# Logit matmuls of two attention units side by side on different TensorE row groups, in a fused two-block transformer kernel

## What is computed

```python
def _token_mixers(h, ...):
    proj = h @ w_in
    a, b, c, d = jnp.split(proj, ...)
    o_a = _mixer_window(a, sink, slopes[:4])      # "win": 4 heads of 64, bias by distance
    o_b = _mixer_mla(b, ...)                      # "mla": 4 heads of 96
    o_c = _mixer_axial(c, ax_q_norm, ax_k_norm)   # "ax": 4 heads of 64
    o_d = _mixer_diff(d, ...)                     # "dif": 4 heads, two maps of 32 each, bias by distance
    return jnp.concatenate([o_a, o_b, o_c, o_d], axis=-1) @ w_out
# every mixer: s = q @ k.T * scale (+ bias); p = softmax(s); o = p @ v
```

## Time and profile before

| | |
|---|---|
| runs (3) | 1475.52, 1479.99, 1492.61 us; median 1479.99 us |
| profiled execution | 1476.0 us |
| its span, first to last instruction | 1474.7 us |
| mean granted TensorE clock | 0.968 |
| busy: TensorE, VectorE, ScalarE, GpSimd | 1389.5, 845.7, 657.8, 93.0 us |

### The profile page before, as it was taken

The page is one execution under the profiler, slowest core; times in us unless marked ns, Lnnn a source line. Parts: engine busy times, 40 slices in busy tenths (PEclk is TensorE's granted clock), DMA queues, the critical chain, the costliest instruction groups (busy, mean ns, idle before and its releaser), DMA issues.

```text
span 1474.7 us, 23294 instructions
## 1 busy us (share of the span) xinstructions
PE 1389.5 (94%) x9838; PEld 1290.4 (88%) x9838; DVE 845.7 (57%) x1141; ACT 657.8 (45%) x939; POOL 93.0 (6%) x137
## 2 busy tenths in 40 slices
PE   6798799999899999998899999899999999899997
PEld 6687799998799998888889999899998878799997
DVE  3787655666655547546554546655457446655545
ACT  5556345445434443555244344443343545344332
POOL 1233000000000000500000000000001400000000
PEclk9998889999999999999899999999999999899999
DMA  7233276667556563421575566566655232376561
GB/s 225 87 95 120 86 214 186 186 187 206 164 180 196 177 186 104 136 94 37 141 220 180 173 195 204 155 189 184 198 153 155 91 114 69 104 209 191 181 197 52
DMA packets 301201, 229.36 MB, mean 156 GB/s; under 512 B 13083, under 2 KB 283818, under 8 KB 301098
## 3 DMA queue, kind: packets, MB, share of 16 engines
q1 hardware_dynamic: 301082, 227.88, 51.3%
q10 hardware_dynamic: 16, 0.00, 0.0%
HBM read 226.80 MB, written 1.05 MB: 155 GB/s over the span
## 4 chain that ended last, share of the span: by engine, by line
PE 82%; DVE 10%; ACT 5%; DMA 1%; issue 1%; POOL 0%; SPq 0%; DVEq 0%; ACTq 0%
PE bank L796 24%; PE bank L797 24%; PE bank L798 24%; DVE lo_gu L1638 3%; PE bank L1213 2%; PE bank L1183 2%; ACT hi_gu L1307 2%; PE bank L1193 1%; PE bank L1000 1%; DVE stats L1665 1%; DMA st_gu<-in_w_out 1%; PE bank L806 1%; PE bank L1010 1%; DVE xTl L1653 1%; DVE x L1659 1%
## 5 line engine op out<-in xcount | busy, mean ns | idle before, releaser
L796 PE MATMUL bank<-xTh,hi_gu 128*128 128x256 f32 x1864 | 533.2, 286 | 9.6 <-DVE big L1843 5.8
L797 PE MATMUL bank<-xTl,hi_gu 128*128 128x256 f32 x1864 | 531.2, 285 | 0.0
L798 PE MATMUL bank<-xTh,lo_gu 128*128 128x256 f32 x1864 | 531.1, 285 | 0.0
L1638 DVE TENSOR_TENSOR lo_gu<-st_gu,hi_gu 128x2048 fp32r<-128x2048 f32 (+2 forms) x146 | 324.1, 2222 | 169.6 <-ACT hi_gu L1307 169.6
L796 PEld LDWEIGHTS bank<-xTh,hi_gu 128*128 128x128 f32 x1864 | 361.8, 194 | 13.6 <-issue 7.8
L797 PEld LDWEIGHTS bank<-xTl,hi_gu 128*128 128x128 f32 x1864 | 361.8, 194 | 1.7
L798 PEld LDWEIGHTS bank<-xTh,lo_gu 128*128 128x128 f32 x1864 | 361.5, 194 | 0.0
L1307 ACT ACTIVATE hi_gu<-st_gu 128x2048 fp32r<-128x2048 f32 (+3 forms) x147 | 269.5, 1837 | 20.7 <-DMA st_gu<-in_ffn_w_val 10.5
L796 PE MATMUL bank<-hi_dn,actTh 128*128 128x512 f32 x436 | 171.7, 394 | 9.3 <-DVE actTl L1773 7.3
L797 PE MATMUL bank<-lo_dn,actTh 128*128 128x512 f32 x436 | 170.3, 391 | 0.0
L798 PE MATMUL bank<-hi_dn,actTl 128*128 128x512 f32 x436 | 169.8, 389 | 0.0
(11 more groups left out here) (261 smaller groups left out, 1496.8 us busy)
## 6 DMA issues: line engine op xcount, KB each, us to landing
st_gu<-in_ffn_w_gu SPq DMA_DIRECT2D x176, 512.0 KB, 5.1
st_dn<-in_ffn_w_down SPq DMA_DIRECT2D x109, 512.0 KB, 6.3
st_gu<-in_w_in SPq DMA_DIRECT2D x23, 1024.0 KB, 5.4
st_gu<-in_w_out SPq DMA_DIRECT2D x12, 1024.0 KB, 5.2
st_gu<-in_ffn_w_gate SPq DMA_DIRECT2D x21, 512.0 KB, 5.0
st_gu<-in_ffn_w_val SPq DMA_DIRECT2D x21, 512.0 KB, 6.3
st_gu<-in_w_in SPq DMA_DIRECT2D x10, 512.0 KB, 4.8
gb<-in_ln_g SPq DMA_DIRECT2D x6, 512.0 KB, 6.6
```

Of the source, the lines that this page charges most:

```text
L796: pe.matmul(o, lhs[0], rhs[0], start=start, stop=False, **kw)
L797: pe.matmul(o, lhs[0], rhs[1], start=False, stop=False, **kw)
L798: return pe.matmul(o, lhs[1], rhs[0], start=False, stop=stop, **kw)
L1638: i = dve.tensor_tensor(low, staged, high.bitcast(F32), ALU.subtract)
```

## The change

`UNITS` now runs over pr inside m: units u and u+1 (u even) are the same tokens with neighbouring pr, so they lie in different row groups, except in mla. `logits(u)` now issues both units u and u+1. It first waits for the banks of both, then issues the four bias matmuls, then the products in the order (z=0, u), (z=0, u+1), (z=1, u), (z=1, u+1). It is called at even steps only. Nothing else is moved: `weighted`, `probabilities` and the loops of the other engines keep their places.

```diff
-UNITS = [(kind, m, pr) for kind in KINDS for pr in range(4 if kind == "dif" else 2) for m in range(M)]
+UNITS = [(kind, m, pr) for kind in KINDS for m in range(M) for pr in range(4 if kind == "dif" else 2)]
...
                 def logits(u):
-                    kind, m, pr = UNITS[u]
-                    b, ts = bank[u % LOGIT_BANKS], slice(m * P, (m + 1) * P)
-                    if u < LOGIT_BANKS:
-
-                        wait_projected(pe, l, 1, 0)
-                        wait_projected(pe, l, 0, 1)
-                    else:
-                        pe.wait_ge(exp_ok.sem, exp_ok[l, u - LOGIT_BANKS])
+
+                    for v in (u, u + 1):
+                        if v < LOGIT_BANKS:
+
+                            wait_projected(pe, l, 1, 0)
+                            wait_projected(pe, l, 0, 1)
+                        else:
+                            pe.wait_ge(exp_ok.sem, exp_ok[l, v - LOGIT_BANKS])
...
                     for z in range(2):
-                        if kind == "mla":
-                            q_, k_ = mlaq[0:96, 2 * pr + z, ts], mlak[0:96, 2 * pr + z, :]
...
-                        t = pe.matmul(b[:, z * S:(z + 1) * S], q_, k_, start=not biased, stop=True, skip_group_check=biased)
-                    t.then_inc(logits_ok.sem, logits_ok.one((l, u)))
+                        for v in (u, u + 1):
+                            pr = UNITS[v][2]
+                            if kind == "mla":
+                                q_, k_ = mlaq[0:96, 2 * pr + z, ts], mlak[0:96, 2 * pr + z, :]
...
+                            t = pe.matmul(bank[v % LOGIT_BANKS][:, z * S:(z + 1) * S], q_, k_, start=not biased, stop=True, skip_group_check=biased)
+                            if z == 1:
+                                t.then_inc(logits_ok.sem, logits_ok.one((l, v)))
...
                 logits(0)
                 half(4, 0)
-                logits(1)
                 half(4, 1)
                 units = len(UNITS)
                 for s in range(units + 1):
-                    if s + 2 < units:
+                    if s + 2 < units and s % 2 == 0:
                         logits(s + 2)
```

More of the change, by code:

```diff
@@ L1167, in logits @@
                         pe.wait_ge(qk_copied.sem, qk_copied[l, "mla", 1, 2])
+                    kind, m, _ = UNITS[u]
+                    ts = slice(m * P, (m + 1) * P)
                     biased = kind in ("win", "dif")
                     if biased:
-                        for z in range(2):
-                            pe.matmul(b[:, z * S:(z + 1) * S], slopes[:, 2 * pr + z if kind == "win" else 4 + pr, :],
-                                      distances[:, m, 0 if kind == "win" else 1, :], start=(z == 0), stop=False, skip_group_check=True)
@@ L1184, in logits @@
-                    t.then_inc(logits_ok.sem, logits_ok.one((l, u)))
+                        for v in (u, u + 1):
+                            pr = UNITS[v][2]
+                            for z in range(2):
+                                pe.matmul(bank[v % LOGIT_BANKS][:, z * S:(z + 1) * S], slopes[:, 2 * pr + z if kind == "win" else 4 + pr, :],
+                                          distances[:, m, 0 if kind == "win" else 1, :], start=(z == 0), stop=False, skip_group_check=True)
+                    for z in range(2):
+                        for v in (u, u + 1):
+                            pr = UNITS[v][2]
+                            if kind == "mla":
+                                q_, k_ = mlaq[0:96, 2 * pr + z, ts], mlak[0:96, 2 * pr + z, :]
+                            elif kind == "dif":
+                                rows_ = slice(32 * pr, 32 * pr + 32)
+                                q_, k_ = difq[rows_, z, ts], difk[rows_, z, :]
+                            else:
+                                rows_ = slice(64 * pr, 64 * pr + 64)
+                                q_, k_ = (winq, axq)[kind == "ax"][rows_, z, ts], (wink, axk)[kind == "ax"][rows_, :]
+                            t = pe.matmul(bank[v % LOGIT_BANKS][:, z * S:(z + 1) * S], q_, k_, start=not biased, stop=True, skip_group_check=biased)
+                            if z == 1:
+                                t.then_inc(logits_ok.sem, logits_ok.one((l, v)))
```

## The result

The changed kernel runs at 1463.39 us (median of 20 runs), the kernel before at 1475.18 us in the same comparison: a ratio of 0.9919, 95% interval 0.9899 to 0.9938. That is 11.8 us or 0.8% faster, where 7.6 us were forecast. The profiled execution took 1463.38 us, its span is 1462.0 us (1474.7 before). The chain that ended last still has these shares by engine

A forecast was written before the change was run, and what follows sets the result against it. TensorE was taken as the bound (82% of the chain), except at the step-11 wait. Per layer 6.7 us kept less 2.9 of new waits gives 3.8, 7.6 in two layers: 1470.0 us, range 1460 to 1485.

The forecast's parts named there:

- A pair costs one unit: Logits on TensorE: two units in different row groups run side by side, eight records lasting as long as four, 1.05 us.
- the bound of no overlap: Upper bound for a pair of logits: eight records one after another, 1.91 us; as a rival, no change, chance 0.13.
- The wait in step 11 takes back two pairs: TensorE's wait behind output chunk 3's load grows to about 5 or 6 us; units 10 to 13 lose 2.3 us saved.
- the rival that more would stay: Step-11 wait falls, new waits are hidden, half clock behind it goes; about 1460 us, over 1% faster, chance 0.14.
- The new waits: Odd steps: TensorE waits for the copy of probabilities in steps 1, 13, 15, 17; 2.9 us per layer, even steps nothing.
- The sum: Per layer 6.7 us kept less 2.9 of waits gives 3.8, two layers 7.6; time taken as 1470.0 us.
- The clock in the mla steps: Rival: waits in mla keep TensorE at 1.2 GHz to step 17, some 13 us per layer, 1498 us; chance 0.07.
- The rival's sentence that the waits would vanish at half clock: In the falling-clock case, steps last twice as long and the waits of 2.2 us vanish; the rival's chance 0.07.
- the reading that the full clock was back at 679 us: Kernel before, after the step-11 wait of 3.7 us: half clock follows, full clock back at 679 us after gapless TensorE work.

The follow-up runs named there:

- mla_single: Changed kernel with the logits of mla (units 16 to 19) issued one at a time at each step, as before; 1461.29 us, ratio to before 0.9907.
- late_chunk_single: Kernel before with output chunk 3 moved later (high part from step 9 to 12, low part to 13); 1465.34 us, ratio 0.9922.
- ax_second_pair_single: Changed kernel with the logits of units 4 and 5 (ax) issued singly in steps 2 and 3; 1478.88 us, ratio to before 1.0015.
- order_alone: Kernel before with only the new UNITS order, still one unit of logits at every step; 1474.48 us, ratio 1.0000.
- pairs_same_rows: Changed kernel's pairs at even steps, but UNITS in the old order, so both units share a row group; 1476.69 us, ratio to before 1.0014.
- aabb_in_pair: Changed kernel, but inside each pair both halves of unit u come first, then both of u+1; 1465.8 us, ratio to before 0.9939.
- ax_single_mla_single: Changed kernel with the logits of units 4 and 5 and of all mla units issued singly; 1465.51 us, ratio to before 0.9928.

## Why the prediction was right, point by point

- **A pair costs one unit.** Right, and exact: 1.07 us where 1.05 was taken, 1.89 without row groups where the bound of no overlap was 1.91. It came from a routine of other shape in the same trace, by subtracting 0.19 us for each change of row groups. That subtraction carried the reading: the 0.42 us of `scores` as they stand are just four records of 0.107 one behind the other, and what backed the overlap besides was only the stretch with four records in flight. No run measures what a change costs inside `scores`. The Trainium skill, "TensorE: Matmul & The Clock Gate", Part 3, has a pack in different row groups last about as long as one of its matmuls. The traces here agree, at 256 float32 columns and two units: 1.07 us against 1.05.
- **The wait in step 11 takes back two pairs.** Right: steps 8 to 12 took 22.1 us before and after, and the pairs save 1.05 us there once the load is out of the way. The wait grew to 4.74 us, a little short of the "5 or 6" forecast. The chain kept its length (14.0 against 14.1). So the rival that more would stay, by the half clock behind that wait, falls: that half clock lasts 6.8 us in both kernels. More did stay than was counted, but in another place.
- **The new waits.** Right in place and size: from start to start 0.69 in step 1, 0.4 to 0.5 in step 13, 0.85 in steps 15 and 17, none at even steps. The profile's own idle times are shorter (0.45, 0.25, 0.69), since part of the latency is filled. mla_single takes the last ones away.
- **The sum.** Too small: 6.1 and 6.3 us per layer against 3.8. Of the difference, 1.5 to 1.6 per layer are the half-clock stretch of step 3 (8.22 us for the step with it in the kernel before, 6.70 without it in late_chunk_single). The prediction read the clock only from 635 us on and never priced this stretch, which stands at 625 to 629 us of the trace that it had. Without it the gain would have been some 8.6 us (an estimate: 11.8 less twice 1.6), close to the 7.6. The remaining 0.7 to 0.8 are small terms: 0.15 in the pairs of steps 0 and 1, 0.1 in each pair of ax, 0.3 in steps 8 to 13 together, and 0.16 in the mla steps, which lost 1.56 and not 1.72. The time itself, 1463.4 against the 1470.0 taken, was off by 6.6: 4.2 from the gain, and 2.4 from the base, which was set between the profiled execution and a median of three runs (1479.99, where 20 runs gave 1475.18).
- **Was the missing stretch the work of the change?** Not shown, so some 3 of the 11.8 us have no shown cause. In ax_second_pair_single, the experiment made for it, the stretch stayed away, and late_chunk_single loses it in one layer with the same instructions. That the stretch stands in both layers of the profiled executions of the kernel before and of order_alone, and in none of the kernels with pairs, speaks for a link; what the link is stays open. It is not the two row groups, since pairs_same_rows has no such stretch in step 3 either. And in four kernels with pairs a stretch of that length stands elsewhere, in steps 6 to 10 of a layer, so it may have moved and not gone.
- **The clock in the mla steps.** As a mechanism it is real, and priced rightly: steps 7 to 19 of ax_second_pair_single take 56.4 us in the layer with it and 44.1 in the other, 12 us more where some 13 were reckoned. That it strikes a kernel one edit away, whose ten runs took 1474 to 1485 us, and mostly not the changed kernel was luck: nothing in the prediction told the two apart. In the changed kernel's profile it does not happen, 0.93 mean clock over the mixers' second half in both layers. The rival's sentence that the waits would vanish at half clock was wrong: they stay at 0.69. So was the reading that the full clock was back at 679 us in the kernel before: it is back at 676.7.

## What to carry to other kernels

Two units of small matmuls on different row groups and banks, issued with nothing between them, took as long as one (1.07 us against 1.05), and their order inside the pair made no difference. Pair only those that really lie in different row groups: for the others the pairing just takes cover from a latency further down, here the copy between two TensorE steps, and it leaves small waits with which the clock can stay low for far longer than the waits are (34 us with waits of 0.69). And before counting a gain on the busiest engine, find the next wait of it that a DMA ends: what is saved between the start of that chain and its end is worth nothing until the chain is moved, and moving it (9 to 11 us) was worth nearly as much as the change itself.

## What the runs showed of the hardware that I had not expected

- Matmuls of two row groups overlap even where the program gives both of one group first (1.07 us a pair in aabb_in_pair). Had the second half of the first unit held up the second unit, the pair would have taken 1.4 to 1.5 us, by the estimate made before that run. The Trainium skill, "TensorE: Matmul & The Clock Gate", Part 3, has matmuls in strict order by start and end; the trace does not agree, and the measurement decides.
- TensorE can stay at 1.2 GHz for 34 us while it is busy for 32.3 of them, in a row of 64- to 256-column matmuls with waits of 0.69 us in every second step. Without these waits, in ax_single_mla_single, half clock lasted 6.8 us and the mean clock of the same steps was 0.85.
- Going into a row group of 32 or 64 rows and out of it costs about 0.19 us, whether four or eight records run inside. Four take 1.05 us where four of 96 rows take 0.87; eight take 1.89 to 1.92 (pairs_same_rows) where eight of 96 rows take 1.73.
